# Banded attention's first eight units placed inside the last two input projections of a hybrid encoder layer

## The reference

```python
h = rmsnorm(x)
aq, ak, av, bq, bk, bv, cin = split(h @ w_in)
o_win  = window_gqa(aq, ak, av, sink, slopes)     # 4 query heads, 2 kv heads, +-128 tokens
o_diff = diff_attention(bq, bk, bv, ...)
o_rwkv = rwkv7_bidir(cin, conv, ...)              # centred 3-tap conv, two scans
x = x + concat(o_win, o_diff, o_rwkv) @ w_out
x = x + cross_attn(rmsnorm(x), rmsnorm(mem));  x = x + swiglu(rmsnorm(x));  out = rmsnorm(x)
```

## Time and profile before

| | us |
|---|---|
| runs of the kernel | 1679.98, 1679.59, 1673.70; median 1679.59 |
| the profiled execution's own time | 1674.48 |
| its span, first to last instruction | 1672.7 |
| PE busy | 1605.2 (96%) |
| DVE, ACT, POOL busy | 805.0, 734.5, 759.3 |
| jobs 10 and 11 (by PE's timeline) | 415.9 to 462.2 |
| stage behind them, to RWKV's first matmul | 462.2 to 527.6 |

### The profile page before, as it was taken

The page is one execution under the profiler, slowest core; times in us unless marked ns, Lnnn a source line. Parts: engine busy times, 40 slices in busy tenths (PEclk is TensorE's granted clock), DMA queues, the critical chain, the costliest instruction groups (busy, mean ns, idle before and its releaser), DMA issues.

```text
span 1672.7 us, 31783 instructions
## 1 busy us (share of the span) xinstructions
PE 1605.2 (96%) x13137; PEld 1324.3 (79%) x13137; DVE 805.0 (48%) x1290; ACT 734.5 (44%) x1389; POOL 759.3 (45%) x670
## 2 busy tenths in 40 slices
PE   7999999999977999989999999999999999999998
PEld 6888878777855778868888878788888888888886
DVE  4104888427364765553432657543343344244336
ACT  5324888643365544333454754223223323322325
POOL 3222665122164733364455015546547556555651
PEclk9999999999979999999999999999999999999999
DMA  6110000121000010017233002112012102111203
GB/s 209 51 50 25 1 1 1 70 70 44 20 0 7 4 54 5 4 64 252 95 106 103 19 14 94 39 51 76 26 51 76 50 27 76 63 38 51 75 2 126
DMA packets 62541, 91.61 MB, mean 55 GB/s; under 512 B 4434, under 2 KB 45552, under 8 KB 62144
## 3 DMA queue, kind: packets, MB, share of 16 engines
q1 hardware_dynamic: 61456, 87.08, 15.5%
q0 software_dynamic: 944, 2.52, 0.6%
HBM read 83.29 MB, written 6.29 MB: 54 GB/s over the span
## 4 chain that ended last, share of the span: by engine, by line
PE 87%; DVE 6%; ACT 3%; issue 2%; POOL 2%; DMA 1%; SPq 0%; DVEq 0%; ACTq 0%; POOLq 0%
PE PS L2696 7%; PE PS L2698 7%; PE PS L2697 7%; PE PS L2329 7%; PE PS L2047 5%; PE PS L2050 5%; PE PS L2048 5%; PE PS L2703 5%; PE PS L2704 5%; PE PS L2705 5%; PE PS L2060 4%; PE PS L2062 4%; PE PS L2061 4%; PE PS L2144 3%; PE PS L2188 3%; PE PS L2401 2%
## 5 line engine op out<-in xcount | busy, mean ns | idle before, releaser
L608 POOL TENSOR_TENSOR WL<-RAW,WH 128x512 fp32r<-128x512 f32 x120 | 170.8, 1434 | 354.1 <-ACT WH L877 353.4
L2047 PE MATMUL PS<-HH,WH 128*128 128x512 f32 x416 | 164.3, 395 | 0.3 <-DVE SM L1465 0.3
L1992 DVE TENSOR_TENSOR X<-PS,X 128x512 f32<-128x512 f32 x160 | 110.6, 692 | 109.1 <-PE PS L2705 109.1
L784 POOL TENSOR_TENSOR WL<-WU_RAW,WH 128x512 fp32r<-128x512 f32 x60 | 77.3, 1296 | 188.6 <-ACT WH L861 188.6
L2048 PE MATMUL PS<-HL,WH 128*128 128x512 f32 x416 | 161.9, 389 | 0.0
L877 ACT ACTIVATE WH<-RAW 128x512 fp32r<-128x512 f32 x121 | 74.3, 630 | 149.5 <-PE PS L2050 54.1
L2703 PE MATMUL PS<-WH,FH 128*128 128x512 f32 x352 | 137.0, 389 | 1.7 <-DVE FL L1946 1.7
L2704 PE MATMUL PS<-WL,FH 128*128 128x512 f32 x352 | 136.9, 389 | 0.0
L2705 PE MATMUL PS<-WH,FL 128*128 128x512 f32 x352 | 136.9, 389 | 0.0
L2050 PE MATMUL PS<-HH,WL 128*128 128x512 f32 x416 | 133.5, 389 | 0.0
L2698 PE MATMUL PS<-HH,WL 128*128 128x512 f32 x320 | 124.5, 389 | 0.0
(11 more groups left out here) (404 smaller groups left out, 3879.9 us busy)
## 6 DMA issues: line engine op xcount, KB each, us to landing
WD_RAW<-in_ffn_w_down SPq DMA_DIRECT2D x44, 256.0 KB, 2.6
RAW<-in_w_in SPq DMA_DIRECT2D x43, 256.0 KB, 2.8
WG_RAW<-in_ffn_w_gu SPq DMA_DIRECT2D x20, 512.0 KB, 4.2
WU_RAW<-in_ffn_w_gu SPq DMA_DIRECT2D x20, 512.0 KB, 4.5
RAW<-in_w_out SPq DMA_DIRECT2D x32, 256.0 KB, 2.7
XT<-in_x SPq DMA_DIRECT2D x8, 512.0 KB, 6.6
X<-in_x SPq DMA_DIRECT2D x8, 512.0 KB, 6.2
RAW<-in_x_wq SPq DMA_DIRECT2D x16, 256.0 KB, 2.7
```

What stands on the lines that cost most here:

```text
L608: pool.tensor_tensor(w_low, raw_at(p), w_high.bitcast(F32), ALU.subtract).then_inc(w_lo, 2 if p < N_VAL else 1)
L784: pool.tensor_tensor(w_low, quarter(kind, i, name), w_high.bitcast(F32), ALU.subtract).then_inc(w_lo, 1)
L2047: pe.matmul(where(ct, i), wh[:, k, c], ah(kt)[:, t0:t0 + n], start=first and starts(ct, i), stop=False, skip_group_check=True)
```

## The change

Unit u is now spread over "places": `w_place(n)` on PE does `w_values(n - 3)`, `w_scores(n)`, `w_turn(n - 2)`. Places 0 to 11 lie between pieces and half pieces of jobs 10 and 11 (`within`, and the new `inside`, called in the middle of a piece), one for each 12 matmuls. Units 0 to 7 are complete there, and `w_scores(8)` too; ACT has the same places. For room, jobs 10 and 11 both use banks 0 to 3, scores of units 0 to 8 one pair of banks (4, 5), the transposes banks 6 and 7, and the values' output half of bank 7. So job 11 waits for all of job 10's copies, and `w_turn` and `w_values` for the copy of the unit before. Pieces 40 to 47 use four slots of the ring in place of six. Outputs of units 0 to 7 go to `OW`, and one new transfer on SP's queue moves them to `MIX`. The biases of the four heads become one table, scaled by the slope in L1676, with queries scaled to match. `conv(4)` and `conv(5)` come behind units 6 and 7. Behind the projections units 9 to 15 run from their scores on, unit 8 from its transposes on, and `v_turned` takes two tiles at a time. What is cut: declarations, tables of names, the same edit at a second place.

```diff
+        WB_ = at("WB_", 206, [384])
+        WPI = [at(f"WPI{i}", b, [2, 384]) for i, b in enumerate((156.03125, 159.03125, 20))]
+        WTI = at("WTI0", 162.03125, [4, 128]), at("WTI1", 23, [2, 128])
+        OW = at("OW", 8, [2, 512])
 
         CV = CIN[:, :, 2:T + 2]
...
 
         def wide_at(p):
...
 
             qb, kv = u // 2, u % 2
...
+        def w_bank(u):
+
+            return 4 if u <= NWI else 2 * (u % 2)
+
+        def weights_of(u):
+
+            return (WPI if u <= NWI else WP_)[u % 3]
+
+        def turned_of(u, i):
+
+            if u >= NWI:
+                return WT_[:, u % 2, i, :]
+            return WTI[i // 4][:, i % 4, :]
+
+        def out_of(u):
+
+            return PS[:, 6, 0:P] if u >= NWI else PS[:, 7, 256:256 + P]
 
 
...
+            sp.wait_ge(w_mix, NWI)
+            sp.wait_ge(r_exp, 5)
+            sp.dma_start(MIX[:, 4:6, 0:512], OW[:, :, :]).then_inc(mix_moved, 16)
             sp.wait_ge(r_kd_used, 6)
-            sp.wait_ge(mix_moved, 32)
+            sp.wait_ge(mix_moved, 48)
...
+            for p in range(30, P_FOUR):
                 lo(p)
-
-            pool.wait_ge(w_lo, 4 * NJ)
-            pool.dma_start(WB_[:, :, :], io["win_bias"].rearrange("p (h k) -> p h k", h=4)).then_inc(tables_in, 16)
+            pool.wait_ge(r_c, 2)
+            pool.dma_start(WB_[:, :], io["win_bias"][:, 0:384]).then_inc(tables_in, 16)
+            for p in range(P_FOUR, P_FOUR + 6):
+                lo(p)
+
+            def w_weigh(u):
+
+                nk, c = window(u)[3], slice(2 * (u % 3), 2 * (u % 3) + 2)
+                pool.wait_ge(w_r, u + 1)
+                pr = weights_of(u)[:, :, 0:nk * P]
+                pool.tensor_tensor(pr, pr, WR[:, c].unsqueeze(2).broadcast_to([P, 2, nk * P]), ALU.mult).then_inc(w_p, 1)
+
+            w_weigh(0)
+            lo(P_FOUR + 6)
+            w_weigh(1)
+            w_weigh(2)
+            lo(P_FOUR + 7)
+            for u in range(3, NWI):
+                w_weigh(u)
+            pool.wait_ge(w_used, 4 * NJ)
+            pool.memset(CIN[:, 4:6, 0:1], 0.0)
+            pool.memset(CIN[:, 4:6, T + 1:T + 2], 0.0).then_inc(pads, 1)
+            w_weigh(NWI)
             def kd_steps():
 
                 pool.wait_ge(w_used, 4 * NJ)
...
             kd0 = kd_steps()
-            for u in range(NWU):
-
-                nk, c = window(u)[3], slice(2 * (u % 3), 2 * (u % 3) + 2)
-                pool.wait_ge(w_r, u + 1)
-                pr = WP_[u % 3][:, :, 0:nk * P]
-                pool.tensor_tensor(pr, pr, WR[:, c].unsqueeze(2).broadcast_to([P, 2, nk * P]), ALU.mult).then_inc(w_p, 1)
-                if u >= 2 and u % 2 == 0:
-                    next(kd0, None)
-                if u == 11:
+            next(kd0)
+            for u in range(NWI + 1, NWU):
+                w_weigh(u)
+                next(kd0, None)
+                if u == 13:
                     pool.wait_ge(r_conv, 8)
                     link(pool.memset(SCM[1][:, :], 1.0))
...
+                if nk == 3:
+                    a = act.activation(rest, PS[:, t0 + 1, 0:256].rearrange("p (k q) -> p k q", k=2), ACT.Copy)
+                a.then_inc(w_pt, 1)
+
+            def w_out_evac(u):
+                qb, kv, _, _ = window(u)
+                act.wait_ge(w_pv, u + 1)
+                t = slice(qb * P, (qb + 1) * P)
+                act.activation(OW[:, kv, t] if u < NWI else MIX[:, 4 + kv, t], out_of(u), ACT.Copy).then_inc(w_mix, 1)
+
+            def w_place(n):
+                if 0 <= n - 3 < NWI:
+                    w_out_evac(n - 3)
+                if 0 <= n - 2 < NWI:
+                    w_turned(n - 2)
+                if n < NWI:
+                    w_exps(n)
+                if n == NWI + 3:
+                    w_exps(NWI)
+
             for j in range(6, NJ):
-                hi(min(4 * j + 10, 4 * NJ))
...
                     for b in range(2):
                         a = act.activation(AV[:, 4 * b:4 * b + 4, :], PS[:, 6 + b, :].rearrange("p (t c) -> p t c", t=4), ACT.Copy)
                     a.then_inc(v_lo, 1)
+                    w_place(0)
+                    w_place(1)
+                    hi(P_FOUR + 7)
+                    w_place(2)
+                    w_place(3)
+                    hi(P_FOUR + 8)
+                if j == J_AK + 2:
+                    for n in range(4, NWI + 4):
+                        w_place(n)
...
+            for u in range(NWI, NWU):
+                if u + 2 < NWU:
                     w_exps(u + 2)
-                act.wait_ge(w_tr, u + 1)
-                if u >= 2:
-                    act.wait_ge(w_pv, u - 1)
-                a = act.activation(WT_[:, u % 2, 0:4, :], PS[:, 4, :].rearrange("p (k q) -> p k q", k=4), ACT.Copy)
-                if nk == 3:
-                    a = act.activation(WT_[:, u % 2, 4:6, :], PS[:, 5, 0:256].rearrange("p (k q) -> p k q", k=2), ACT.Copy)
-                a.then_inc(w_pt, 1)
-                if u == 0:
+                w_turned(u)
+                if u == NWI:
                     for ct in range(2):
                         decay_exp(ct, KR[:, 1, ct], -E05)
-                if u == 1:
+                if u == NWI + 1:
                     for ct in range(2):
                         decay_exp(ct, BKt[:, 0, ct], E05)
                     act.activation(DD[0].rearrange("p (a c) -> p a c", a=2), S1_[:, :, C - 1:T:C], ACT.Exp, scale=-E05).then_inc(r_exp, 1)
                     act.wait_ge(r_exp, 5)
-                if u:
+                if u > NWI:
                     w_out_evac(u - 1)
             w_out_evac(NWU - 1)
+            act.wait_ge(mix_moved, 48)
 
             r_sigmoids(1, (0,))
...
+                dve.tensor_copy(VT[:, 2 * q:2 * q + 2, :], PS[:, 7, :].rearrange("p (t c) -> p t c", t=2)).then_inc(r_vte, 1)
+
+            for u in range(NWI):
+                if u:
...
+                    w_norm(u - 1)
                 w_max(u)
-                w_norm(u)
-            w_max(2)
-            w_norm(2)
-            for u in range(NWU):
-                if 3 <= u + 2 < NWU:
+                if u == 6:
+                    conv(4)
+            w_norm(NWI - 1)
+            conv(5)
+            w_max(NWI)
+            w_norm(NWI)
+            w_max(NWI + 1)
+            w_norm(NWI + 1)
+            dve.wait_ge(pads, 2)
+            for u in range(NWI, NWU):
+                if u + 2 < NWU:
                     w_max(u + 2)
-                if 3 <= u + 1 < NWU:
-                    w_norm(u + 1)
-                if u < 2:
-                    conv(6 + u)
-                elif u < 4:
-                    first_keys(u - 2)
+                    w_norm(u + 2)
+                if u < 10:
+                    conv(6 + u - 8)
                 elif u < 12:
-                    v_turned(u - 4)
-                if u in (9, 13):
-                    r_keys((u - 9) // 4)
+                    first_keys(u - 10)
+                if 11 <= u < 15:
+                    v_turned(u - 11)
+                if u in (12, 14):
+                    r_keys((u - 12) // 2)
             dve.wait_ge(tables_in, 48)
 
...
                 if j == 2:
                     pe.wait_ge(vec_c, 1)
-                pe.wait_ge(job_evac, 4 * (j - 1))
-                c0, bank = proj_cols[j], 4 * (j % 2)
-                feature_job(4, hh, hl, lambda ct, i: PS[:, bank + 2 * ct + i, :], after=after)
+                pe.wait_ge(job_evac, 4 * j if j > J_AK + 1 else 4 * (j - 1))
+                bank = job_bank(j)
+                feature_job(4, hh, hl, lambda ct, i: PS[:, bank + 2 * ct + i, :], after=after, between=between)
...
-            def window_values(q):
+            def w_turn(u):
+                nk, bank = window(u)[3], 6 if u < NWI else 4
+                pe.wait_ge(w_p, u + 1)
+                if u:
+                    pe.wait_ge(w_pt, u)
+                    pe.wait_ge(w_mix, min(u, NWI))
+                else:
+                    pe.wait_ge(v_lo, N_VAL // 2 + 1)
+                for g in range(2):
+                    for k in range(nk):
+                        i = nk * g + k
+                        mm = pe.transpose(PS[:, bank + i // 4, P * (i % 4):P * (i % 4) + P], weights_of(u)[:, g, k * P:(k + 1) * P], ID)
+                mm.then_inc(w_tr, 1)
+
+            def w_values(u):
+
+                _, kv, first, nk = window(u)
+                pe.wait_ge(w_pt, u + 1)
+                if u:
+                    pe.wait_ge(w_mix, u)
+                for k in range(nk):
+                    for g in range(2):
+                        mm = pe.matmul(out_of(u)[64 * g:64 * g + 64], AV[:, first + k, 64 * kv:64 * kv + 64], turned_of(u, nk * g + k),
+                                       start=k == 0, stop=k == nk - 1, skip_group_check=True)
+                mm.then_inc(w_pv, 1)
+
+            def w_place(n):
+                if 0 <= n - 3 < NWI:
+                    w_values(n - 3)
+                if n < NWI:
+                    w_scores(n)
+                if n == NWI + 3:
+                    w_scores(NWI)
```

(51 more changed lines are left out.)

114 lines of the change are left out of this document (53 added, 61 removed).

## The result

The changed kernel takes 1691.70 us in the median (four runs, 1690.47 to 1692.57), the kernel before in the same comparison 1678.37 (four runs). The ratio is 1.0082, 95% interval 1.0062 to 1.0102: slower by 0.8%, some 13 us. Its profiled execution took 1692.01 us with a span of 1690.2, that is 17.5 above the span before.

What follows compares the result with a forecast made beforehand. PE, busy 1605.2 of 1672.7 us, was taken to bound the kernel, the stage behind the projections being bound by latency. 15.7 + 2.7 - 13.6 = +4.8 on 1679.6 gave 1684, range 1673 to 1696.

Steps and rivals of the forecast that it cites:

- rival B: In the projections: PE waits about 1 us at each of nine places, adding 8 to 9 us; 1693, chance 0.20.
- a stage over 57 us: Behind the projections: a stage this long would show the forecast wrong; 50 to 54 us would show it right.
- Work added to the projections: In the last projection jobs: PE work of the moved units, +15.7 us, between 14 and 17.
- Waits added there: In the projections: PE waits of 1.8 at the job border and twice 0.45 in places 8 and 9, +2.7 us.
- The start of the stage: Behind the projections: the first maximum starts 3.5 us behind the last projection matmul.
- DVE's rounds: Behind the projections: seven units of 3.3 us each on DVE, about 1.9 of each waiting; 23.1 us.
- rival A: Behind the projections: DVE's wait for the Exps is covered, 13 us fall out; 1671, chance 0.11.
- Collisions: Behind the projections: GpSimd in the way of DVE's steps, 2.0 us, between 0 and 7.
- The end of the stage: Behind the projections: the last copy of turned values waits for PE, 1.9 us.
- rival C: PE's clock falls to 1.2 GHz for the last units and first scan steps, slowing them: +4, 1688, chance 0.12.
- The scans: RWKV's scans behind the stage: the forecast had 0 for any change there.
- -13.6: The stage behind the projections: falls from 65.4 us to a sum of 51.8, between 46 and 57.

Runs made afterwards that it cites:

- e3: Values of units 0 to 7 cut to one block of keys: in the changed kernel 1687.16 us, in the kernel before 1678.15 us.
- e1: Changed kernel with DVE's norm of each unit put behind the next unit's maximum, as before the change: median 1685.44 us, ratio 1.0028.
- e8: e7 with GpSimd's key steps replaced by memsets to zero as well, leaving out part of the computation: one run, 1678.94 us.
- e2: Changed kernel with GpSimd's six big key steps replaced by memsets to zero: one run, 1687.44 us.
- e5: Changed kernel with e1's order and scores of units 9 to 15 computed three times over: median 1685.75 us, ratio 1.0030.
- e7: Changed kernel with e1's order, and weights of units 9 to 15 multiplied on ScalarE in place of GpSimd: median 1686.25 us, ratio 1.0037.
- e6: Kernel before with 56 small matmuls added between and behind the last three scan steps: median 1685.13 us, ratio 1.0035.
- e4: Changed kernel, scores computed four times and turns twice behind the projections: 1695.15 us; kernel before, scores of units 3 to 15 computed twice: 1679.95 us.

## Why the prediction was right or wrong, step by step

The time of 1691.7 lies in the range of 1673 to 1696, but on the slower side, 7.7 above the forecast of 1684, and the kernel is slower beyond the 0.5% that was given the most weight as "same". The difference to the kernel before was forecast as +4.8 and came to +13.3. It lies in the range by luck in part: the upper end of 1696 was rival B's, and B did not happen. By the prediction's own sign, a stage over 57 us, its sum for the stage was wrong.

- **Work added to the projections, +15.7: right, a little low;** 16.8 with the waits taken off and a start 0.4 later. A place of 12 projection matmuls, values, scores and turn takes 5.13 (449.74 to 454.87). The 12 alone take 2.76 in the kernel before, so a unit costs 2.37 and not 2.26. The scores take 0.81 where they stand behind values, against 0.71 behind projection matmuls (478.54 to 479.25 in the changed kernel too); the turn takes 0.57 in place of 0.75, but the 12 matmuls between two places 2.95 in place of 2.76 (451.92 to 454.87). Six units make 0.7 of it; PE also came to the first of these steps 0.4 later (427.18 in place of 426.82), and 0.4 stays without a row. e3 shows that such work is paid for there (3.3 for 3.7) and was free before.
- **Waits added there, +2.7: right.** 1.8 and twice 0.47, with the releaser named. Rival B fell: ordinary places don't wait.
- **The start of the stage, 3.5: right,** 3.32.
- **DVE's rounds, 23.1: the mechanism right.** Undisturbed rounds took 3.26 (509.87 to 513.13), the narrow ones 2.8. With what GpSimd did to three of them the seven came to 24.6, without it they would be 21.9. e1 shows that the waits in them were the path: rival A's gain of some 10 us was there to be had, by an order that this change doesn't have, and that the kernel before had.
- **Collisions, +2.0: the step that failed.** They came to 8.2: 2.8 in the rounds, 4.9 in the two convolutions, 0.5 in `r_keys`. That is above even the upper bound of 7. A further 2.3, in `first_keys`, had been in its row already and was taken for the step's own price; e8 shows it is not. I had weighed one collision of 1.05 from the earlier trace rows and taken two of them, though the list puts a multiply of the weights on GpSimd right behind every norm, just where DVE's largest steps start, and the key steps right behind the multiply.
- **The end of the stage, 1.9: low.** The wait was 2.7, and after the last DVE step 1.1 went by until RWKV's first matmul, which I had not counted. Unit 13 is a wide one, so its values cost 0.80 and not the 0.53 of a narrow unit, and at the low clock they took 1.14. The same seven blocks would need some 5.5 us by full-clock rows of these kernels (an estimate: 0.56, 0.80, 0.41, 0.59, 0.59, 1.91, 0.59), and took 7.05: some 1.6 of rival C's mechanism was there, in the last units, where the forecast had nothing for it.
- **The scans, 0: not shown to be wrong.** The +3.7 of the profiled executions is no larger than the scatter: 209.8, 212.3 and 214.1 with the order of the kernel before, 213.5, 214.1, 212.1 and 211.8 with that of the changed one, and the medians leave nothing for it. Rival C's other sign was seen in part. In the first 60 us the clock was 0.97 in place of 1.00, with 1648 records in place of 1695; it was 0.97 in e2 too, but 1.00 in e3's changed kernel.

Stated as the prediction's own sum: -13.6 was -6.7. Of the 6.9 between them the collisions are 6.2; the end of the stage is 1.9 and `r_keys` with the last copies 0.2, less some 1.2 that the narrow and undisturbed rounds were cheaper and 0.2 at the start. (The 2.25 that the prediction names for PE's start in the kernel before is 2.15 in the earlier trace rows; no sum uses it.)

The rule cited beside the collisions, from the Trainium skill, SBUF — State Buffer, Who interferes with whom, was the better guide: DVE and GpSimd take the shared port pair as an exclusive lock for a whole instruction, and a DVE instruction with two SBUF inputs contends only with a GpSimd instruction that reads SBUF. By it the sum would have been +9.8, as the prediction had it as an estimate. The traces agree in both parts: steps of DVE with two SBUF inputs waited for the rest of GpSimd's instruction and then ran (1.29 alone, 2.37 and 3.26 beside it), and the GpSimd memsets of e2 and e8 held none of them. They also show GpSimd held: its 1.47 us multiply of weights took 1.89 in the rows above.

The rule on the other side, from the Trainium skill, Perfetto Trace Analysis, Optimization Strategy, says that interleaving regimes bound by different engines may gain; here it gained nothing. e3 shows why in two numbers: 3.7 us of PE work costs 3.3 in the projections and nothing behind them. Work that was hidden was moved to where nothing hides it.

No version of the changed kernel that computes the whole result beats the kernel before. The nearest, e1, e5 and e7, stand at 1.0028 to 1.0037 of it.

## What to carry to other kernels

Before moving work from a stage with idle PE into one with a full PE, price it at the full rate in the new place and at zero in the old one, and ask what else the shorter stage frees: here it was DVE's list that bound the changed stage up to the last units, and PE's own list from there, so taking half of PE's units out gave back little. A step that waits for another engine, as the norm does, is worth trying one item later in an in-order list; here that order alone was worth 10 us of a stage of 59. And a DVE step's price read in one place holds only if GpSimd was quiet there: look at GpSimd's row beside it before the number is multiplied.

## What the runs showed of the hardware that I had not expected

**A two-column DVE instruction can be held for a microsecond.** The minimum (L1679), 0.16 us when alone, took 1.16, 0.57 and 1.10 beside GpSimd's reads, and 1.26 once in the kernel before (at 484.53). It stands between the maximum and the Exps, so ACT waited as well.

**Collisions depend on how GpSimd's work is packed.** The same key steps stretched one convolution to 8.1 us when they followed one another (e7), and two to 6.5 and 5.3 when the multiplies lay between them (e1).

**PE's clock counts where PE's list ends a stage.** PE's last run, from unit 14's turn to RWKV's first matmul, is the same work in the changed kernel, e1, e2, e7 and e8. It took 7.05 us at a mean granted clock of 0.76, 7.00 at 0.76, 8.23 at 0.63, 8.34 at 0.62 and 7.00 at 0.76. A mean over the whole stage doesn't tell this: e7's is 0.76, above the 0.68 of the changed kernel.

**The scans differ from one execution to the next by as much as the whole effect.** They do the same 6175 matmul records in every kernel but e6. Where the granted clock was 0.98 or 0.99 over them they took 208.8 to 212.3 us; at 0.96 and 0.97, 211.8 to 214.1; at 0.95, in e8, 217.5; at 0.94, in e1 and e7, 220.7, e1's stretches of 20 us being between 0.74 and 1.00. PE is 94% busy in that stretch. Run by run the same is seen in the mean clock of the whole execution: 50 runs of the kernel before lie between 1673.15 us at 0.991 and 1685.26 at 0.983, e1's between 1677.85 at 0.988 and 1690.93 at 0.980.

Between kernels the mean clock is a poor guide, since the low clock of the stage counts in it: the median run of the kernel before had 0.988, of the changed kernel 0.981, but e4's changed kernel had 0.988 too and was as slow, at 1695.15. By projections and stage alone e1 and e7 would lie 2.9 and 3.3 us above the kernel before; the ratios say 4.7 and 6.2, a difference inside their intervals. So no loss in the scans is shown for any of the changed kernels, and what sets the clock there the runs do not say. One profiled execution can mislead by as much as the whole effect, as e5's did.
